# A depthwise convolution moved from VectorE and GpSimd to TensorE, as matmuls with diagonal matrices

## The reference

```
def conformer_conv(u, dw, ln_g, ln_b, pw):
    a, gate = jnp.split(u, 2, axis=-1)
    h = a * jax.nn.sigmoid(gate)
    h = depthwise_conv(h, dw)          # 31 taps, each channel by itself
    h = jax.nn.silu(layernorm(h, ln_g, ln_b))
    return h @ pw
```

## Time and profile before

| | |
|---|---|
| median of three runs | 3670.92 us (3665.43 to 3671.42) |
| the profiled execution | 3665.97 us |
| its span in the profile | 3664.7 us |
| PE, DVE, ACT, POOL busy | 90%, 61%, 48%, 6% of the span |
| mixers | about 1292 to 1540 us and 2475 to 2720 us |

### The profile page before, as it was taken

How to read it: one execution, slowest core, us unless ns; L and a number is a source line. 1 busy time by engine, 2 the same in 40 slices (tenths; PEclk the granted TensorE clock), 3 DMA queues, 4 the chain that set the end, 5 groups by cost and what they waited for, 6 DMA issues and landing times.

```text
span 3664.7 us, 52201 instructions
## 1 busy us (share of the span) xinstructions
PE 3314.5 (90%) x19560; PEld 2812.7 (77%) x19560; DVE 2223.3 (61%) x4465; ACT 1768.6 (48%) x3736; POOL 225.0 (6%) x290
## 2 busy tenths in 40 slices
PE   7799899999889977898699999997789869999999
PEld 3375578877569976797578999987589758999998
DVE  6733543333666565568966666667457886666665
ACT  6732433322345433532955555553442395555554
POOL 0001200000110035000000000004400000000000
PEclk9988989998889977799999999998789999999999
DMA  8830022332215622343055666662134305566564
GB/s 310 301 106 24 13 69 92 92 90 71 64 59 184 200 76 59 93 150 121 1 162 186 187 184 184 185 208 96 42 113 146 104 1 184 184 186 188 184 186 153
DMA packets 134932, 479.99 MB, mean 131 GB/s; under 512 B 15385, under 2 KB 17305, under 8 KB 133913
## 3 DMA queue, kind: packets, MB, share of 16 engines
q1 hardware_dynamic: 132080, 467.59, 40.5%
q10 hardware_dynamic: 2600, 9.04, 0.7%
HBM read 475.53 MB, written 1.05 MB: 130 GB/s over the span
## 4 chain that ended last, share of the span: by engine, by line
PE 81%; DVE 9%; issue 3%; ACT 3%; DMA 3%; ACTq 0%; DVEq 0%
PE psum L646 14%; PE psum L648 14%; PE psum L647 14%; PE psum L2252 7%; PE psum L2253 7%; PE psum L2254 7%; PE psum L2174 6%; PE psum L2098 4%; PE psum L507 3%; DMA raw<-in_mod_w 3%; DVE w_lo L229 2%; PE psum L915 1%; PE psum L519 1%; DVE conv_part L1383 1%; ACT prob L1021 1%
## 5 line engine op out<-in xcount | busy, mean ns | idle before, releaser
L229 DVE TENSOR_TENSOR w_lo<-raw,w_hi 128x512 fp32r<-128x512 f32 x1664 | 1133.5, 698 | 795.8 <-ACT w_hi L220 766.8
L220 ACT ACTIVATE w_hi<-raw 128x512 fp32r<-128x512 f32 x1664 | 1010.6, 626 | 869.2 <-PE psum L648 658.9
L646 PE MATMUL psum<-x_hi,w_hi 128*128 128x256 f32 x2096 | 600.3, 286 | 34.5 <-DVE w_lo L229 27.3
L648 PE MATMUL psum<-x_hi,w_lo 128*128 128x256 f32 x2096 | 597.0, 285 | 0.0
L647 PE MATMUL psum<-x_lo,w_hi 128*128 128x256 f32 x2096 | 596.6, 285 | 0.0
L646 PEld LDWEIGHTS psum<-x_hi,w_hi 128*128 128x128 f32 x2096 | 401.4, 192 | 47.2 <-DVE w_lo L229 29.7
L2252 PE MATMUL psum<-w_hi,wt_hi 128*128 128x512 f32 x1024 | 406.5, 397 | 6.5 <-DVE wt_lo L2310 6.5
L647 PEld LDWEIGHTS psum<-x_lo,w_hi 128*128 128x128 f32 x2096 | 401.2, 191 | 7.9
L2253 PE MATMUL psum<-w_lo,wt_hi 128*128 128x512 f32 x1024 | 406.6, 397 | 0.0
L2254 PE MATMUL psum<-w_hi,wt_lo 128*128 128x512 f32 x1024 | 405.4, 396 | 0.0
L648 PEld LDWEIGHTS psum<-x_hi,w_lo 128*128 128x128 f32 x2096 | 400.3, 191 | 0.0
(11 more groups left out here) (324 smaller groups left out, 4867.8 us busy)
## 6 DMA issues: line engine op xcount, KB each, us to landing
raw<-in_v SPq DMA_DIRECT2D x256, 512.0 KB, 4.2
raw<-in_u SPq DMA_DIRECT2D x190, 512.0 KB, 3.5
raw<-in_mod_w SPq DMA_DIRECT2D x96, 512.0 KB, 4.8
raw<-in_w_gate_up SPq DMA_DIRECT2D x88, 512.0 KB, 3.5
u_raw<-in_u SPq DMA_DIRECT2D x66, 512.0 KB, 3.5
raw<-in_w_in SPq DMA_DIRECT2D x40, 512.0 KB, 3.7
raw<-in_w_down SPq DMA_DIRECT2D x32, 512.0 KB, 3.5
raw<-in_w_peer SPq DMA_DIRECT2D x32, 512.0 KB, 3.7
```

Source lines behind the costliest of these rows:

```text
L220: self.nc.scalar.activation(self.hi[:, m % 4, :], self.half(m), ACT.Copy).then_inc(self.rounded[m % 4], 1)
L229: self.nc.vector.tensor_tensor(self.lo[:, m % 4, :], self.half(m), self.hi[:, m % 4, :], ALU.subtract).then_inc(self.ready[m % 4], 1)
L646: pe.matmul(out[:, 0:width], hi[:, w], x_hi, start=(c == 0), stop=False)
L648: mm = pe.matmul(out[:, 0:width], lo[:, w], x_hi, start=False, stop=(c == total - 1))
```

## The change

All 31 taps of both halves are made on TensorE. The matmul of a diagonal matrix, with the 128 weights of a tap on its diagonal, by the shifted input is the tap's product, and PSUM adds the 31 up. GpSimd makes the 62 diagonal matrices from the identity (`gpsimd_diagonals`), in a ring of 16, each signalled to TensorE, which signals its use back. TensorE runs the taps in groups behind the tiles of the projections: six matmuls behind each of tiles 7 to 11 of `first`, four behind each tile of `mem_kv` and of `second`. The sum takes PSUM bank 3, so `first`, `second` and `third` rotate over three banks in place of four. ScalarE copies the sum to `conv` behind `third`. VectorE's taps, its join and GpSimd's taps go.

```
-        self.uses = [k.bank[b0 + n % 4].use(written=0) for n in range(len(self.tiles))]
+        self.uses = [k.bank[b0 + n % banks].use(written=0) for n in range(len(self.tiles))]
...
             product(k, use.tensor, self.cuts, self.x, self.width, self.arrive if n == 0 else None)
+            if self.between is not None:
+                self.between.tensor_between(n)
...
-    def vector_taps(self, first, last):
-
-        k, dve = self.k, self.k.nc.vector
+    def tensor_taps(self, first, last):
+
+        pe, use = self.k.nc.tensor, self.conv_use
         if first == 0:
-            dve.wait_ge(*self.gated.after(1))
...
+            pe.wait_ge(*self.gated.after(1))
+            pe.wait_ge(*use.free())
+        for n in range(first, last):
+            j, c = divmod(n, 2)
+            pe.wait_ge(*self.diag_made.after(n + 1))
+            pe.matmul(use.tensor[:, c * LAT:(c + 1) * LAT], self.diag[:, n % self.DIAGONALS, :],
+                      self.pad[:, 0, c, j:j + LAT], start=(n == 0), stop=(j == self.TAPS - 1),
+                      skip_group_check=True).then_inc(self.diag_used.sem, 1)
+
+    def scalar_conv(self):
+        act = self.k.nc.scalar
+        act.wait_ge(*self.diag_used.after(2 * self.TAPS))
+        act.activation(flat(self.conv[:]), self.conv_use.tensor[:], ACT.Copy).then_inc(self.conv_use.read.sem, 1)
...
-    def gpsimd_conv(self):
+    def gpsimd_diagonals(self):
         k, pool = self.k, self.k.nc.gpsimd
-        pool.wait_ge(*self.gated.after(1))
-        self.depthwise(self.conv[:], self.pad[:, 0], G_CONV, self.TAPS, self.VECTOR_TAPS)
-        pool.tensor_copy(self.tap[:, 0, 0, 0:1], self.conv[:, 0, 0:1]).then_inc(self.conv_made.sem, 1)
+        for n in range(2 * self.TAPS):
+            j, c = divmod(n, 2)
+            if n >= self.DIAGONALS:
+                pool.wait_ge(*self.diag_used.after(n - self.DIAGONALS + 1))
+            pool.tensor_scalar(self.diag[:, n % self.DIAGONALS, :], k.ident, self.weight(G_CONV, c, self.TAPS, j), 1.0,
+                               ALU.mult, ALU.mult).then_inc(self.diag_made.sem, 1)
...
+                                 between=Taps(self.branches, [(30 + 4 * n, 34 + 4 * n) for n in range(4)]))
...
+        self.second = ScalarProjection(k, io[f"w_in{l}"], [0, 1, 10, 11], [DC], xs, LAT, place, banks=3,
+                                       between=Taps(self.branches, [(46 + 4 * n, 50 + 4 * n) for n in range(4)]))
...
-        if n > 5:
-            self.branches.vector_taps(2 * (n - 6), 2 * (n - 5))
+
+    def tensor_between(self, n):
+        if n >= 7:
+            self.branches.tensor_taps(6 * (n - 7), 6 * (n - 6))
...
-        pe.wait_ge(*self.joined.after(1))
+        pe.wait_ge(*self.branches.conv_use.emptied())
...
         self.third.scalar()
+        self.branches.scalar_conv()
...
-        self.branches.vector_join().then_inc(self.joined.sem, 1)
```

More of the change, by code:

```diff
@@ L653, with __init__ @@
 class Projection:
-    def __init__(self, k, w, tiles, cuts, x, width, place, arrive=None, b0=0, scale=lambda t: 1.0, between=None):
+    def __init__(self, k, w, tiles, cuts, x, width, place, arrive=None, b0=0, scale=lambda t: 1.0, between=None, banks=4):
         self.scale, self.between = scale, between
@@ L702, in vector, with __init__, scalar_between, vector_between @@
                 self.between.vector_between(n)
+class Taps:
+    def __init__(self, branches, taps):
+        self.branches, self.taps = branches, taps
+    def scalar_between(self, n): ...
+    def vector_between(self, n): ...
+    def tensor_between(self, n):
+        if n < len(self.taps):
+            self.branches.tensor_taps(*self.taps[n])
 class ScalarProjection(Projection):
@@ L1328, with __init__ @@
 class Branches:
-    VECTOR_TAPS = 12
     TAPS = 31
-    def __init__(self, k, l, proj, y, pad, work, pooled, conv, conv_part, tap, pool_w, inv_count):
+    DIAGONALS = 16
+    def __init__(self, k, l, proj, y, pad, work, pooled, conv, diag, tap, pool_w, inv_count):
         self.k, self.l, self.proj, self.y, self.pad, self.work = k, l, proj, y, pad, work
-        self.pooled, self.conv, self.conv_part, self.tap = pooled, conv, conv_part, tap
+        self.pooled, self.conv, self.diag, self.tap = pooled, conv, diag, tap
         self.pool_w, self.inv_count = pool_w, inv_count
@@ L1341, in __init__ @@
         self.gated = k.named("conv_input_gated").take(1)
-        self.part_made = k.named("conv_part_made").take(1)
-        self.conv_made = k.named("conv_made").take(1)
+        self.diag_made = k.named("diagonals_made").take(2 * self.TAPS)
+        self.diag_used = k.named("diagonals_used").take(2 * self.TAPS)
+        self.conv_use = k.bank[3].use(written=0)
         self.pool_ready = k.named("pooled").take(1)
@@ L1780, in __init__ @@
         drow, mrow = k.sb("diff_v", [P, 2, GW], 34816), k.sb("mem_v", [P, 2, GW], 36864)
-        conv_part, tap = k.sb("conv_part", [P, 2, LAT], 38912), k.sb("tap", [P, 2, 2, LAT], 40960)
+        diag = k.sb("diagonals", [P, Branches.DIAGONALS, P], 38912)
+        tap = k.sb("tap", [P, 2, 2, LAT], 63488)
         m_hi, m_lo = k.sb("m_hi", [P, DC, LAT], 47104, F32R), k.sb("m_lo", [P, DC, LAT], 55296, F32R)
@@ L1801, in __init__ @@
                            (flat(lamp[:]), io["lam"][l:l + 1, :].to_broadcast([P, P])))
+        self.branches = Branches(k, l, proj, y, pad, work, pooled, conv, diag, tap, pool_w, inv_count)
         mem = [memT[:, c, :] for c in range(DC)]
@@ L1827, in __init__ @@
                               head(proj[:, 16:18, :], HD, mq), head(mk[:], HD, k.gain(l, G_MK))], (4, 5, 7, 6))
-        self.second = ScalarProjection(k, io[f"w_in{l}"], [0, 1, 10, 11], [DC], xs, LAT, place)
-        self.branches = Branches(k, l, proj, y, pad, work, pooled, conv, conv_part, tap, pool_w, inv_count)
-        self.third = ScalarProjection(k, io[f"w_in{l}"], [12, 13, 14, 15], [DC], xs, LAT, place)
-        self.mean, self.mean_row = k.bank[7].use(), conv_part[:, 0, :]
-        self.joined = k.named("conv_joined").take(1)
+        self.second = ScalarProjection(k, io[f"w_in{l}"], [0, 1, 10, 11], [DC], xs, LAT, place, banks=3,
+                                       between=Taps(self.branches, [(46 + 4 * n, 50 + 4 * n) for n in range(4)]))
+        self.third = ScalarProjection(k, io[f"w_in{l}"], [12, 13, 14, 15], [DC], xs, LAT, place, banks=3)
+        self.mean, self.mean_row = k.bank[7].use(), k.sb("mean_row", [P, LAT], 38912)[:]
         self.centred = k.named("conv_centred").take(2)
@@ L1965, in gpsimd @@
         self.branches.clear(self.start)
-        self.branches.gpsimd_conv()
+        self.branches.gpsimd_diagonals()
         self.branches.gpsimd_pool(self.second.done)
```

22 lines of the change are left out of this document (3 added, 19 removed).

## The result

| | before | with the change |
|---|---|---|
| median of five runs each | 3670.92 us (3665.43 to 3672.08) | 3688.53 us (3685.96 to 3691.47) |
| ratio of the two, 95% interval | | 1.0047 (1.0035 to 1.0059) |
| profiled execution, its span | 3665.97, 3664.7 | 3691.47, 3689.9 |
| from the first matmul behind the gate's wait to the mean, mixer 1 and 2 | 83.61, 83.63 | 93.55, 92.60 |

The change makes the kernel 17.6 us slower by the medians. The last line is the measure that the rest of this text uses. It runs from the second half of tile 7 of `first` to the mean, holds all that the change alters in the queues of TensorE and VectorE (GpSimd makes the first 16 diagonals before it), and grows by 9.94 and 8.97 us, 18.9 us together.

What follows compares the result with a forecast made beforehand. The prediction took TensorE as the bound, with VectorE setting the pace around the change. Per mixer 6.0 + 5.2 - 0.6 = +10.6 us, twice +21.2, less clock gain +19.5, gave 3688 us; range 3682 to 3696, widened 3674 to 3701.

Steps and rivals of the forecast that it cites:

- A tap of 0.432 us: On TensorE, a float32 tap matmul takes two passes of 0.216 us at full clock; 62 taps are 26.8 us per mixer.
- The first stretch: From the gate to the transposes, 46 taps replace waits and slow clock; the transposes start 6.0 us later, at clock 1.00.
- The rival of the falling clock: The clock falls in the first stretch all the same, costing 3 us a mixer again: +25.5 us, 3694; chance 0.12.
- `second`, +5.2: In second, 16 taps cost 6.9 us, of which 1.7 us is covered by the spread's wait: net +5.2 us.
- Behind `third`, -0.6: The join leaves VectorE's queue ahead of the mean, -0.6 us; ScalarE's copy of the sum from PSUM costs nothing.
- Clock behind the spread: The clock's fall after the spread's wait may go, up to 1.7 us a mixer; half of it was taken.
- GpSimd, 0.37 us a diagonal: GpSimd makes each diagonal in 0.37 us, against 1.5 us available for each refill, so TensorE never waits.
- Three banks free: In second, three PSUM banks in place of four are enough, since each tile is evicted while the next is computed.
- Cheap taps: Rival: a pass of 0.12 us suffices on TensorE, 62 taps take 7.4 us and the kernel gets faster, 3652; chance 0.05.
- Late GpSimd: Rival: TensorE waits for diagonals from 1.5 us each; at 2 us, +20 us a mixer, 3728; chance 0.03.
- priced increments: Rival: each tap's increment and wait cost up to 0.1 us on TensorE's path, up to +12 us, 3700; chance 0.08.
- More clock back: Rival: slow clock at 1388 to 1400 and 1408 to 1416 us goes, returning 5 us a mixer; within 0.2%, chance 0.07.

Runs made afterwards that it cites:

- e4: The changed kernel with diagonals and convolution input rounded to float32r, so a tap is one pass, in a ring of 8 diagonals: 3659.61 us, 0.9965 of before.
- e3: The kernel before, with first, second and third on three PSUM banks and nothing else changed: 3673.60 us, 1.0002 of before.
- e2: The changed kernel with one signal and one wait for each two tap matmuls in place of one for each: 3691.05 us, 1.0050 of before.
- e7: The changed kernel with only 2 of its 62 tap matmuls per mixer, the other 60 and their diagonals left out: 3647.45 us, 0.9939 of before.
- e1: The changed kernel with 32 of its 62 tap matmuls per mixer, spread over the same tiles: 3670.91 us, 0.9991 of before.
- e12: The changed kernel with only 18 tap matmuls per mixer, all behind tiles 7 to 9 of first, where TensorE doesn't wait: 3663.82 us, 0.9976 of before.
- e10: The changed kernel with only 18 tap matmuls per mixer, 2 in the work and 16 in TensorE's waits: 3642.75 us, 0.9920 of before.
- e11: All 31 taps on three engines: seven on TensorE in its waits, five on VectorE, 19 on GpSimd as in the kernel before: 3647.83 us, 0.9932 of before.
- e8: e4 with its last 16 taps placed in waits, 2 and 4 behind the transposes, 10 ahead of the spread: 3654.01 us, 0.9951 of before.
- e9: The kernel before with VectorE's 12 taps one by one behind tiles of first (six), mem_kv (one), second (four) and third (one): 3654.24 us, 0.9953 of before.

## Why the prediction was right

3688 was predicted, 3688.53 measured. By its own steps:

**A tap of 0.432 us, two records of 0.216.** Right: 2.59 us for twelve records. e4, at 0.119 us, is faster than before, so the price of float32 operands decides the sign.

**The first stretch, transposes 6.0 us later.** Right where its condition held: 6.04 us in the second mixer (44.39 against 38.35), at clock 1.00. In the first mixer it was 7.6 us. The rival of the falling clock happened there: behind the gate's wait of 2.46 us, PEclk was 0.75 in the next 6.8 us, which is 3.4 us at half clock and 1.7 us lost.

```profile
1349.20:1356.00 6.80, 6.80 (x34) 6.29 (x35) 2.85 (x5) 0.63 (x1) 2.60 (x6) 0.75 0.65 210
```

**`second`, +5.2, and the spread's wait near 2.1.** In the second mixer the wait was 2.10 us, as said. In the first it was 1.17, and the piece from the transposes to the spread grew by 4.2 and 5.1 us, so the second one is the prediction's 5.2. The clock is 0.89 in both; the difference is VectorE's first copy for the spread. In the first mixer it took 0.43 us:

```profile
1424.43 0.43 DVE L483 COPY spread<-mean_col 128x512 f32<-128x512 f32 x1
...
1424.43 1.37 POOL L1463 TENSOR_TENSOR work<-work 128x538 f32<-128x538 f32 x1
```

and in the second 1.35:

```profile
2615.91 1.35 DVE L483 COPY spread<-mean_col 128x512 f32<-128x512 f32 x1
...
2615.90 1.08 POOL L1463 TENSOR_TENSOR work<-work 128x538 f32<-128x538 f32 x1
```

The copy and a sum of GpSimd's pooling come due within 0.01 us of each other, and the copy is short or long; the whole 0.92 us goes to TensorE. Before, it took 1.35 us too, so of the 2.65 us by which the first mixer's wait shrank 0.9 us is this and not the taps.

**Behind `third`, -0.6, ScalarE's copy free.** Right: the mean's wait is 2.14 us for 2.74, and ScalarE's copy stands beside VectorE's applies and ends before the last of them begins:

```profile
1440.91 0.59 ACT L1405 ACTIVATE conv<-psum 128x512 f32<-128x512 f32 x1
...
1442.50 0.74 DVE L566 SCALAR_TENSOR_TENSOR mem_k<-mem_k,gvec,psum 128x512 f32<-128x512 f32 x1
```

**Clock behind the spread, half of 1.7 us.** Mis-sized: from the spread to the mean PEclk rose from 0.92 to 1.00 in both mixers, and the piece shrank by 1.84 and 2.17 us, of which 0.6 is the join. The gain is 1.2 and 1.6 us, not 0.85.

**GpSimd, 0.37 us a diagonal.** Right: 372 ns, and TensorE waits for none.

**Three banks free; increments and waits free.** Right by e3 and e2. The rule of the Trainium skill, TensorE: Matmul & The Clock Gate, section "The cost: per-tile semaphore tail", would have the 62 increments that e2 leaves out cost some 1.6 us, an estimate at the page's 26 ns each (31 in a mixer, 0.8 us). The stretches of e2 differ from those of after by 0.04 us at most. The trace does not agree for these matmuls, which last 0.432 us each and follow each other in one queue; the page's own case, small matmuls packed side by side, isn't in this kernel.

**The sum.** Predicted +19.5 us, measured +18.9 in the two stretches and +17.6 by the medians. It came out this well partly because two terms of it were too large by nearly the same. e7 and the kernel after it separate them. What goes (waits, slow clock, join) was put at 13.1 + 0.6 = 13.7 us a mixer; e7, with its two taps taken off at 0.9 us, gives 11.8 and 10.5. What comes was put at 26.8 - 1.7 - 0.75 - 0.85 = 23.5 us; after against e7, with those two taps added, gives 21.8 and 19.5. The common cause is the step that took the clock as 1.00 in one piece and left it unchanged in the others: with the waits gone and nothing in their place, the clock falls more between transposes and spread (e7), and with taps among them it falls less (after). As the change does both, most of it cancels. Someone who had used the same prices for e7 or e4 alone would have been wrong by 5 us and more, since a float32 matmul taken out along the whole stretch gave back 0.31 to 0.40 us (e7 and e1, two mixers each), not the 0.432 that e12 pays behind the gate, and e4 gave back 12.7 and 14.9 us of 19.4.

**The rivals.** Cheap taps: refuted by 2.59 us for six. Late GpSimd and priced increments: refuted. More clock back: true behind the spread, where PEclk is 1.00, and not between the transposes and the spread, where 6.5 us at half clock are left of 7.2 (PEclk 0.89 for 29.77 us, against 0.86 for 25.61). The fallen clock: true in one mixer of two, so its price came to 1.7 us and not 6.

Of the 25.5 us between the two profiled executions, 18.9 are in the two stretches. The rest lies where TensorE has the same instructions in both kernels; the last section shows how far such executions differ.

## What to carry to other kernels

Work moved to the engine that bounds the program pays only up to the waits it removes; price it by what a matmul of its type takes, before anything else (here 0.432 against 0.119 us decided the sign). First try the same work elsewhere in the same queue: one tap a tile in place of two gave 16 us for nothing, and 16 matmuls a mixer put exactly where TensorE waits cost nothing that the ratios show, where the same 16 in the work cost 0.432 us each. Count a wait on TensorE with the clock that follows it, and compare variants by a stretch that both have, since the profiled executions differ elsewhere.

## What the runs showed of the hardware

**More matmuls, and no more time.** e10 issues 16 float32 matmuls more per mixer than e7 and its stretches are 4.2 and 2.5 us shorter. 5.9 us of waits were filled with 6.9 us of work, so that alone would make it 1 us longer; the clock gives 5.2 and 3.9 us back (half of 13.1 - 2.7 and of 17.8 - 10.0 us at half clock). That is one execution of each; by several runs the ratios are 0.9920 (0.9905 to 0.9934) and 0.9939 (0.9923 to 0.9954), so that e10 is faster is likely but not shown.

**The same wait, another clock.** The gate's wait is 2.46 us in both mixers of the changed kernel. Behind it the clock was 0.75 for 6.8 us in the first and 1.00 in the second, with the same instructions. In e3 the same stretch took 88.08 and 83.53 us, in e4 the same piece 29.83 and 26.95. So one profiled execution says little about a clock-bound difference of less than 5 us in one mixer; two mixers and the medians of several runs do.

**Identical programs are not in step.** Up to the first mixer all these kernels issue the same work, and yet the matmul behind the gate's wait starts at 1336.25 us in e12 and 1350.71 in e3, 14.5 us apart, in single executions (1304.13 and 1317.29 us already at the first matmul of `first`). Against that, the 6.6 us (25.5 - 18.9) which the profiled executions of before and after differ by outside the stretches are nothing to explain.

**VectorE beside GpSimd.** A remainder takes 694 ns on average without the convolution on GpSimd and 890 with it; in e11 a single one reached 1.50 us. The copy for the spread takes 0.43 or 1.35 us in the changed kernel where it starts within 0.01 us of GpSimd's sum; when the copy is the short one, GpSimd's sum takes 1.37 us and not 1.08. In both pairs shown here one of the two is the longer for it. As the spread waits for this copy, 0.7 to 0.9 us between two kernels there can be this alone, as in e8 and e9.
